# Two blocks of a transformer: x before the memory tokens at the start, and the second memory projection inside the waits of the normalizer and router

## What is computed

```python
for layer in range(2):
    mem_kv = mem @ w_mem_kv[layer]                # 256 memory tokens -> 256 key and 256 value columns
    h = x @ a_w_in[0]                             # layer 0: q, f_raw, i_in, g (768 columns each), qm (256)
    seq_out = hgrn2_mix(q, f_raw, i_in, g, ...)   # gated linear recurrence
    mem_out = memory_attention(qm, mem_k, mem_v)
    x = post_norm(x, concat(seq_out, mem_out) @ w_o[layer], ...)   # layer norm of 2**0.5 * x + y
    x = post_norm(x, hier_moe(x, ...), ...)       # top group of 4, top 2 experts of 4 in it
```

## Time and profile before

| | us |
|---|---|
| median of 3 runs | 1787.0 (1785.41 to 1790.78) |
| profiled execution, device time | 1784.4 |
| its span in the trace | 1782.7 |
| PE busy in it | 1706.0 (96%) |
| mean granted PE clock | 0.982 of full |

### The profile page before, as it was taken

How to read it: one execution, slowest core, us unless ns; L and a number is a source line. 1 busy time by engine, 2 the same in 40 slices (tenths; PEclk the granted TensorE clock), 3 DMA queues, 4 the chain that set the end, 5 groups by cost and what they waited for, 6 DMA issues and landing times.

```text
span 1782.7 us, 28889 instructions
## 1 busy us (share of the span) xinstructions
PE 1706.0 (96%) x11796; PEld 1569.2 (88%) x11796; DVE 1064.6 (60%) x1365; ACT 888.1 (50%) x1222; POOL 82.7 (5%) x127
## 2 busy tenths in 40 slices
PE   7999999999989999989999989999999999999998
PEld 6997799878977998779998978999899998989997
DVE  4775676878556668875445555555555556755454
ACT  4645446765554467644445654444544445444443
POOL 8000020003000200000000000000000000000000
PEclk9999999999989999999999999999999999999999
DMA  7530577974204779845553333555455554545552
GB/s 242 167 128 38 172 241 244 339 268 159 102 1 149 238 241 335 272 154 189 188 188 113 118 142 126 183 186 188 142 194 184 188 189 147 184 142 189 188 184 76
DMA packets 236750, 317.24 MB, mean 178 GB/s; under 512 B 5561, under 2 KB 210704, under 8 KB 236656
## 3 DMA queue, kind: packets, MB, share of 16 engines
q1 hardware_dynamic: 234080, 309.09, 52.7%
q0 software_dynamic: 2576, 6.83, 1.4%
HBM read 314.84 MB, written 1.06 MB: 177 GB/s over the span
## 4 chain that ended last, share of the span: by engine, by line
PE 87%; DVE 7%; ACT 3%; issue 1%; DMA 1%; SPq 0%; DVEq 0%; ACTq 0%
PE PB L371 17%; PE PB L372 17%; PE PB L373 17%; PE Y L371 7%; PE Y L372 7%; PE Y L373 7%; PE PB L555 2%; PE PB L556 2%; PE PB L557 2%; DVE LO L1504 2%; ACT HI L998 1%; PE Y L731 1%; PE PB L437 1%; PE PB L641 1%; DVE ST L1570 1%
## 5 line engine op out<-in xcount | busy, mean ns | idle before, releaser
L1504 DVE TENSOR_TENSOR LO<-RAW,HI 128x1024 fp32r<-128x1024 f32 (+2 forms) x498 | 582.0, 1214 | 301.2 <-ACT HI L998 300.6
L371 PE MATMUL PB<-XTH,HI 128*128 128x256 f32 x2128 | 609.4, 286 | 14.5 <-DVE XTL L1543 7.0
L372 PE MATMUL PB<-XTL,HI 128*128 128x256 f32 x2128 | 606.9, 285 | 0.0
L373 PE MATMUL PB<-XTH,LO 128*128 128x256 f32 x2128 | 606.6, 285 | 0.0
L998 ACT ACTIVATE HI<-RAW 128x1024 fp32r<-128x1024 f32 (+2 forms) x498 | 489.1, 1034 | 228.1 <-PE PB L373 173.3
L371 PEld LDWEIGHTS PB<-XTH,HI 128*128 128x128 f32 x2128 | 413.2, 194 | 19.6 <-DVE XTL L1543 8.1
L372 PEld LDWEIGHTS PB<-XTL,HI 128*128 128x128 f32 x2128 | 413.4, 194 | 1.6
L373 PEld LDWEIGHTS PB<-XTH,LO 128*128 128x128 f32 x2128 | 413.1, 194 | 0.0
L371 PE MATMUL Y<-HI,HH 128*128 128x512 f32 x384 | 150.2, 391 | 1.1 <-DVE HL L1514 1.1
L372 PE MATMUL Y<-LO,HH 128*128 128x512 f32 x384 | 150.0, 391 | 0.0
L373 PE MATMUL Y<-HI,HL 128*128 128x512 f32 x384 | 149.4, 389 | 0.0
(11 more groups left out here) (414 smaller groups left out, 2411.6 us busy)
## 6 DMA issues: line engine op xcount, KB each, us to landing
RAW<-in_ffn_pre_w_gate SPq DMA_DIRECT2D x22, 1024.0 KB, 5.3
RAW<-in_ffn_pre_w_up SPq DMA_DIRECT2D x22, 1024.0 KB, 5.3
RAW<-in_ffn_pre_w_down SPq DMA_DIRECT2D x22, 1024.0 KB, 4.8
RAW<-in_ffn_post_w_gate SPq DMA_DIRECT2D x22, 1024.0 KB, 5.3
RAW<-in_ffn_post_w_up SPq DMA_DIRECT2D x22, 1024.0 KB, 5.3
RAW<-in_ffn_post_w_down SPq DMA_DIRECT2D x22, 1024.0 KB, 4.8
AR<-in_w_gate SPq DMA_DIRECT2D x18, 1024.0 KB, 6.7
RAW<-in_w_down SPq DMA_DIRECT2D x18, 1024.0 KB, 5.3
```

The source lines that it names most:

```text
L371: pe.matmul(out_ap, ah, bh, start=start, stop=False)
L372: pe.matmul(out_ap, ah, bl, start=False, stop=False)
L373: return pe.matmul(out_ap, al, bh, start=False, stop=stop)
L1504: ins = dve.tensor_tensor(LO[:, slot, c], raw_of(n.u)[0][:, c], HI[:, slot, c].bitcast(F32), ALU.subtract)
```

## The change

x is loaded and transposed first, in two DMAs; the first weight unit is split ahead of x's evictions. The memory tokens are loaded behind the three f_raw units, and transposed two columns at a time (`mem_pair`) behind the second and third q unit, side unit 0 and side unit 1; the parameters follow side unit 2. Side units 7 and 8 are now w_mem_kv[0]. The two units of w_mem_kv[1] come behind w_o: half of the first in the normalizer's wait in place of 12 of 16 idle products, its other half and the second unit in the router's wait of layer 0 in place of the 15. ACT and DVE split these two units between the operations of the output projection. In both layers the gates are turned after the gather's fifth step, not its eighth.

```diff
 z_full sp_act sp_ready la_full ea_done am_ready so_full log_a
-rt_full r_dve r_act gt_ready gt_sb oh_ready gi_ready sel_ready xg_full xg_f xg_hi xg_lo gw_full gw_sb cnt_full ht_full st_ready yg_full yg_hi yg_lo y_last
+rt_full r_dve r_act gt_ready gt_sb oh_ready gi_ready sel_ready xg_full xg_f xg_hi xg_lo gw_full gw_sb cnt_full y_read mk_done ht_full st_ready yg_full yg_hi yg_lo y_last
 h_mul h_gb h_hi h_lo
...
     for t in range(NT):
-        sp.dma_start(XN[:, t, :], a["mem"][0, t * P:(t + 1) * P, :]).then_inc(s["mem_in"], 16)
-    load_cols(a["w_mem_kv"][0], 0, KC, 0, UC)
-    load_cols(a["w_mem_kv"][0], 0, KC, UC, UC)
-    sp.dma_start(X[:, :, :], a["x"][0].rearrange("(t p) n -> p t n", p=P)).then_inc(s["x_in"], 16)
+        sp.dma_start(X[:, t, :], a["x"][0, t * P:(t + 1) * P, :]).then_inc(s["x_in"], 16)
     for base in (MIX, 0, 2 * MIX):
...
             load_cols(a["a_w_in"][0], 0, KC, base + j * UC, UC)
+        if base == MIX:
+            for t in range(NT):
+                sp.dma_start(XN[:, t, :], a["mem"][0, t * P:(t + 1) * P, :]).then_inc(s["mem_in"], 16)
     load_cols(a["a_w_in"][0], 0, KC, 4 * MIX, UC)
...
         load_cols(a["a_w_in"][0], 0, KC, 3 * MIX + j * UC, UC)
+    load_cols(a["w_mem_kv"][0], 0, KC, 0, UC)
+    load_cols(a["w_mem_kv"][0], 0, KC, UC, UC)
+    load_rows(a["w_o"][0])
     load_cols(a["w_mem_kv"][1], 0, KC, 0, UC)
     load_cols(a["w_mem_kv"][1], 0, KC, UC, UC)
-    load_rows(a["w_o"][0])
     moe(0)
...
+    def cols_half(slot, j):
+        for k in range(KC):
+            w = slice(k * UC + j * P, k * UC + j * P + P)
+            mm = split_product(Y[:, 0, 512 + j * S:512 + (j + 1) * S], HI[:, slot, w], LO[:, slot, w],
+                               CTH[:, k, :], CTL[:, k, :], k == 0, k == KC - 1)
+        return mm
     def moe(layer):
...
         if layer == 0:
-            pe.matmul(Y[:, 1, 0:P], ONES[:, :], TRIL[:, :], start=True, stop=True)
+            pe.matmul(Y[:, 1, P:2 * P], ONES[:, :], TRIL[:, :], start=True, stop=True)
         stay_awake(3, Y[:, 1, 512:1024])
...
             for t in range(NT):
-                mm = pe.matmul(Y[:, 0, t * 512:t * 512 + 20],
+                mm = pe.matmul(Y[:, t, 0:20],
                                TMP[k // 2][:, (k % 2) * S + t * P:(k % 2) * S + (t + 1) * P], RWR[:, layer, k, :],
...
+        if layer == 0:
+            cols_half(mk_slot, 1).then_inc(s["w_used"], 1)
+            claim(0)
+            cols_N(0, **cols_T_mem)
         for b in range(4):
             claim(b, counted=False)
-        stay_awake(15)
+        if layer:
+            stay_awake(15)
         pe.wait_ge(s["sel_ready"], layer + 1)
...
-        gather(range(KC))
+        gather(range(5))
         pe.wait_ge(s["gt_ready"], layer + 1)
...
         mm.then_inc(s["rt_full"], 1)
+        gather(range(5, KC))
...
                 yclaim(1)
+                if layer == 0:
+                    pe.wait_ge(s["mk_done"], 1)
                 pe.wait_ge(s["gt_sb"], layer + 1)
...
     pe.wait_ge(s["ident"], 1)
-    transposes(XN, "mem_in", (32, 32))
     cols_T_mem = dict(xh=CTH, xl=CTL)
-    claim(0)
-    cols_T(0, new=True, **cols_T_mem)
-    claim(1)
-    cols_N(1, **cols_T_mem)
-    pe.wait_ge(s["par_in"], 16 * 12)
-    for b, rows_ in ((2, 70), (3, 85)):
+    transposes(X, "x_in", (32, 32))
+    def mem_pair(i, b):
         claim(b)
-        pe.transpose(PB[:, b, 0:rows_], SM[0:rows_, (b - 2) * P:(b - 1) * P], IDENT[0:rows_, 0:rows_])\
-            .then_inc(s["tp_full"], 1)
-    transposes(X, "x_in", (16, 16))
+        for t in range(NT):
+            for c in range(2):
+                mm = pe.transpose(PB[:, b, c * S + t * P:c * S + (t + 1) * P],
+                                  XN[:, t, (2 * i + c) * P:(2 * i + c + 1) * P], IDENT[:, :])
+        mm.then_inc(s["tp_full"], 1)
+    def parameters():
+        claim(2)
+        pe.wait_ge(s["par_in"], 16 * 12)
+        pe.transpose(PB[:, 2, 0:70], SM[0:70, 0:P], IDENT[0:70, 0:70])
+        pe.transpose(PB[:, 2, 70:155], SM[0:85, P:2 * P], IDENT[0:85, 0:85]).then_inc(s["tp_full"], 1)
     for j in range(6):
...
         cols_T(j % 4, new=j == 0)
+        if j == 4:
+            pe.wait_ge(s["lf_done"], 3)
+            pe.wait_ge(s["mem_in"], 32)
+            mem_pair(0, 2)
+        elif j == 5:
+            mem_pair(1, 3)
...
     side_unit(0)
+    mem_pair(2, 0)
     pe.wait_ge(s["q_ready"], 1)
...
             side_unit(m - 1)
+        if m == 2:
+            mem_pair(3, 1)
+        elif m == 3:
+            parameters()
         pe.wait_ge(s["m_high"], m - 1)
...
             level(m, [(j * P, blk(M, 2 * j), blk(M, 2 * j + 1)) for j in range(6)])
+    read(1)
     mem_scores(0, QM0, (0, 1))
...
     out_rows(first=3, between=mem_beside(0, PN0, PT0), ah=XTH, al=XTL)
-    renewed(16)
+    mk_slot = unit()
+    pe.wait_ge(s["y_read"], 1)
+    cols_half(mk_slot, 0)
+    renewed(4)
     moe(0)
...
         table(SILU_SET)
+        if layer == 0:
+            used()
+            act.activation(MK[:, 1, :, :], Y[:, 0, 512:1024], ACT.Copy).then_inc(s["mk_done"], 1)
+            used()
+            act.activation(MV[:, 1, :, :], PB[:, 0, :], ACT.Copy).then_inc(p_free[0], 1)
         gather_scaled(range(4))
...
     full = [(b, 2 * b, 512) for b in range(4)]
-    transposed(CTH, full)
-    split(RING)
-    used()
-    act.activation(MK[:, 0, :, :], PB[:, 0, :], ACT.Copy).then_inc(p_free[0], 1)
     split()
-    used()
-    act.activation(MV[:, 0, :, :], PB[:, 1, :], ACT.Copy).then_inc(p_free[1], 1)
-    split()
-    act.wait_ge(s["tp_full"], n.next("tp", 2))
-    act.activation(PV[:, 0:70], PB[:, 2, 0:70], ACT.Copy).then_inc(p_free[2], 1)
-    act.activation(PV[:, 70:155], PB[:, 3, 0:85], ACT.Copy).then_inc(p_free[3], 1)
     transposed(XTH, full)
+    split(RING - 1)
+    def mem_pair(i, b):
+        transposed(CTH, [(b, 2 * i, 512)])
+    def parameters():
+        act.wait_ge(s["tp_full"], n.next("tp"))
+        act.activation(PV[:, 0:155], PB[:, 2, 0:155], ACT.Copy).then_inc(p_free[2], 1)
...
             .then_inc(p_free[(3 + j) % 4], 1)
+        if j:
+            mem_pair(j - 1, 1 + j)
         split()
...
         else:
-            ins = act.activation((MK, MV)[j - 7][:, 1, :, :], PB[:, b, :], ACT.Copy)
+            ins = act.activation((MK, MV)[j - 7][:, 0, :, :], PB[:, b, :], ACT.Copy)
         ins.then_inc(p_free[b], 1)
...
     side_unit(0)
+    mem_pair(2, 0)
     def level_exp(m):
...
         side_unit(m - 1)
+        if m == 2:
+            mem_pair(3, 1)
+        elif m == 3:
+            parameters()
         if m == 8:
...
         mem_transposed(PT, (2, 3))
+        if k == 1:
+            split()
         act.wait_ge(s["ao_full"], k)
...
         used()
+        if k == 1:
+            split()
         n.v += 1
...
-        dve.wait_ge(s["x_ready"] if n.at("xr") else s["x_in"], n.at("xr") or 16)
+        dve.wait_ge(s["x_ready"] if n.at("xr") else s["x_in"], n.at("xr") or 32)
         for t in range(NT):
             tile_done(t, experts)
-            after(dve.scalar_tensor_tensor(out=XN[:, t, :], in0=X[:, t, :], scalar=ALPHA, in1=Y[:, t, :],
-                                           op0=ALU.mult, op1=ALU.add))
+            dve.scalar_tensor_tensor(out=XN[:, t, :], in0=X[:, t, :], scalar=ALPHA, in1=Y[:, t, :],
+                                     op0=ALU.mult, op1=ALU.add).then_inc(s["y_read"], 1)
+            dve.wait_ge(s["y_read"], n.next("yr"))
             for h in range(2):
...
-    def mem_and_rows(hi=CTH, lo=CTL):
+    def mem_and_rows(hi=CTH, lo=CTL, more=False):
         used()
...
         used()
+        if more:
+            split()
         mixed(6, PB[:, 0, :], hi, lo)
         used()
+        if more:
+            split()
...
         lg = sm(0, NT, 20)
-        after(dve.tensor_tensor(lg, Y[:, 0, :].rearrange("p (t e) -> p t e", t=NT)[:, :, 0:20],
+        after(dve.tensor_tensor(lg, Y[:, :, 0:20],
                                 bc(RB[:, layer, :].unsqueeze(1), NT, 20), ALU.add))
...
         if layer == 0:
-            after(dve.tensor_copy(IOTA[:, :], Y[:, 1, 0:P]))
+            after(dve.tensor_copy(IOTA[:, :], Y[:, 1, P:2 * P]))
...
+        if layer == 0:
+            n.v += 2
         split()
...
-    n.next("tp", 2)
-    transposed(CTH, CTL)
-    n.next("tp", 4)
-    split(RING)
-    for _ in range(2):
-        used()
-        split()
+    split()
     transposed(XTH, XTL)
-    n.next("tp", 4)
+    n.next("tp", 9)
+    split(RING - 1)
+    def mem_pair(i, b):
+        dve.wait_ge(s["tp_hi"], n.next("tph"))
+        rest(CTL[:, 2 * i:2 * i + 2, :], PB[:, b, :], CTH[:, 2 * i:2 * i + 2, :]).then_inc(p_free[b], 1)
     dve.wait_ge(s["pool_const"], 1)
...
         used()
+        if j:
+            mem_pair(j - 1, 1 + j)
         split()
...
     split()
+    mem_pair(2, 0)
...
             used()
+            if m == 2:
+                mem_pair(3, 1)
             split()
...
     mem_norms(PN0, (3,))
-    mem_and_rows(XTH, XTL)
+    mem_and_rows(XTH, XTL, True)
```

## The result

The changed kernel takes 1764.8 us (median of 4 runs, 1763.7 to 1767.5), against 1786.2 (1779.1 to 1790.8) for the kernel before in the same comparison: ratio 0.9886, 95% interval 0.9851 to 0.9921. The medians differ by 21.4 us, where 18.6 was forecast, and 1764.8 lies within the forecast's own spread, 1764 to 1772.

A forecast was written before the change was run, and what follows sets the result against it. PE was taken as the bound, busy 1706.0 of 1782.7 us. The terms summed to 18.6 us gained, from a median of 1787.0 to 1768; own spread 1764 to 1772, with (a) and (b) 1762 to 1776.

The forecast's parts named there:

- start, to the end of side unit 0: Kernel head: x's first projection starts at 14.15 us and ends at 21.45 against 39.37, +17.9 us gained.
- pair 2's remainder on the level chain: First level: DVE takes this remainder ahead of `differences`, on the chain ending PE's 0.68 us wait; -0.6 us.
- split ahead of the layer norm: Output projection: the second extra unit's split on DVE falls ahead of the layer norm; -0.6 us.
- router of layer 0, to the first expert product: Added projection starts the gather 4.6 us later, the first expert product at 216.7 against 213.97; -2.7 us.
- clock behind the gather, layer 0: First two expert units: without the 1.84 us gap no low clock follows; mean of two layers' losses, +2.0 us.
- the 7.3: Head: us from first product to release of ACT's MK copy in the old first unit, assumed for the new one.
- (a): Behind the gathers: the clock falls anyway, after twelve tiny products; gain 14.6 us, 1772; chance 0.22.
- (b): Layer 0's router: added work exposed whole, and pair 3's 2.1 us comes through; gain 15.3, 1772; chance 0.15.
- pair 3's 2.1: Level chain: pair 3's remainder makes DVE's LO 2.1 us later; forecast hidden, with 0.7 us to spare.
- (c): First units: DVE and ACT bound them, GpSimd's masks slowing LO by 8%; 1.5 us over three units, 1770; chance 0.04.
- (d): Start: no change, the weight stream holds it and PE waits for units instead of x; 1787; chance 0.03.
- (e): Ahead of the layer norm: slower, DVE stuck at the second w_mem_kv[1] unit's split; 1792 at 24 us late; chance 0.04.

The follow-up runs named there:

- run 4: The changed kernel executed once more, unaltered, on the same chip as the three follow-ups before it: 1764.75 us, ratio 0.9904 to the kernel before.
- run 9: The changed kernel with DVE's remainder of memory pair 2 moved behind the first `m_high` product: 1764.65 us, ratio 0.9887.
- run 7: The changed kernel with both halves of the first moved unit in the normalizer's wait, no idle products there: 1763.1 us, ratio 0.9883.
- run 2: The changed kernel with the gates turned after the gather's eighth step again, in both layers: 1770.6 us, ratio 0.9943.
- run 1: The kernel before with only the gates turned after the gather's fifth step, in both layers: 1775.9 us, ratio 0.9962.
- run 3: The changed kernel without the 96 products on the w_mem_kv[1] units, idle products instead: median 1764.9 us of four runs; two others took 2631 and 4206.
- run 5: The changed kernel without PE's claim of bank 0 ahead of layer 0's gather: 1764.9 us, ratio 0.9893.
- run 10: The changed kernel with no bank 0 claim, x's evictions first, both halves in the normalizer's wait, pair 2's remainder late: 1762.5 us, ratio 0.9872.
- run 6: The changed kernel with x's evictions ahead of the first unit's split on ACT and DVE: 1764.25 us, ratio 0.9884.
- run 8: The changed kernel with no bank 0 claim, x's evictions first and both halves in the normalizer's wait: 1763.0 us, ratio 0.9866.

## Why the prediction was right

Its terms against the profiled executions, each the change of the distance between two instructions.

| term | predicted | measured |
|---|---|---|
| start, to the end of side unit 0 | +17.9 | +16.7 |
| memory pairs 0 and 1 | -1.0 | -0.9 |
| pair 2's remainder on the level chain | -0.6 | -0.6 |
| parameters | -0.3 | -0.2 |
| split ahead of the layer norm | -0.6 | -0.7 |
| router of layer 0, to the first expert product | -2.7 | -2.6 in run 4; -6.9 here, with 4.3 of low clock |
| clock behind the gather, layer 0 | +2.0 | +1.5 |
| gates early, layer 1 | +1.9 | +2.1 |
| clock behind the gather, layer 1 | +2.0 | +2.7 |

With run 4's router they add up to 18.0, against 18.6 predicted. The profile after loses the 4.3 in its router, and gains 3.1 at places that the change doesn't touch: 2.3 between the first experts and layer 1's norm, where the granted clock averaged 0.98 against 0.97 before, and 0.9 behind layer 1. That makes 16.9. The 4.3 was in no term of the sum, and that 3.1 came back elsewhere is luck: over the twelve profiles the first of these places took 308.7 to 314.5 us and the second 1193.3 to 1197.3. The ratios of the two comparisons of this kernel, 0.9886 and 0.9904, make 20.4 and 17.1 us, to either side of 18.0.

**The start** was mis-sized by 1.2 us. PE started at 14.06 as forecast (14.15). But the prediction let the new first unit pay "the 7.3" of the old one. It took 22.64 - 14.06 = 8.6, since the granted clock stayed at 0.50 to nearly 20 us. The rule of the Trainium skill (TensorE: Matmul & The Clock Gate, "What's actually happening") that the array starts throttled is borne out again by the 0.55 of the first product. How long it stays so was not in the row of one execution: from the first product to the first eviction it took 7.5 us in run 9 and 8.8 in run 4, with the same work. (Run 9's profile gives a granted clock of 1.00 there, though its first product also took 0.55; so only its time is used.)

**The levels.** The wait for the scaled q is 0.61 where 1.05 stood, since pair 2's transposes now run in it. At the first `m_high` 0.84 stands where 0.68 stood. The prediction had said about 1.3: 0.68 and the 0.6 of pair 2's remainder. That is about what lies between the side unit and the level, but pair 3's four transposes at 67.55 fill part of it, as the prediction's own text on pair 3 had said. At the second `m_high` PE waits for nothing, as predicted. The level starts at 77.67, right behind the parameters, and its operand was ready at 76.4:
```profile
75.44 0.95 DVE L2042 TENSOR_TENSOR AR<-AR 128x768 f32<-128x768 f32 x1
```
So pair 3's remainder stayed hidden. Run 9 settles that pair 2's is the cause of the 0.6.

**The normalizer.** In the changed kernel's DVE timeline the split ends right where the layer norm starts, as predicted.
```profile
165.21 2.36 DVE L1558 TENSOR_TENSOR LO<-RAW,HI 128x1024 fp32r<-128x1024 f32 x2 [4.12 <-ACT HI L1037]
167.49 1.21 DVE L1621 SCALAR_TENSOR_TENSOR XN<-X,Y 128x1024 f32<-128x1024 f32 x1
```
DVE starts the norm 0.7 us later against PE, and PE has no more to do than before, so 0.77 us stay unfilled ahead of its transposes where 0.25 did. This is part of why run 7 gains.

**The router.** The placement was right: the projection costs 4.75 to 4.80 at the gather (4.6 predicted) and 2.64 at the expert unit, since the early gates take out the last split's wait.

**The clock behind the gathers.** The two units take 11.80 or 11.81 us in every one of the twenty places with early gates, so the gain of 1.5 + 2.7 is what the one profile of before had lost. That it came to the 4.0 of the sum is therefore partly luck. In run 2 one place of two with the same gap lost nothing, and the other 1.45.

**The rivals.** (a), a clock that falls behind the gather even without a gap, did not come: no kernel with early gates shows it, in twenty places. The gap was followed by a low clock in both layers of before and in layer 1 of run 2, not in layer 0 of run 2. The old head had such a place too: behind the 2.89 us ahead of x's transposes the granted clock was 0.50 to 0.54 from 30 to 33 us. (b) did not come either: the early gates take 2.1 of the router's 4.75 back, as priced, and pair 3's 2.1 does not come through. (c) is not seen: after 14.06, PE waits for no split in its first units. (d) and (e) are excluded by the ratio.

**What stays open.** No run has the new head alone: its gain is read as distances in the profiles, and only the gates, the projection, pair 2 and the small edits were changed singly. The low stretch in the first router is in the profiles of the changed kernel and of runs 1, 2, 3, 5 and 10, not in those of before and of runs 4, 6, 7, 8 and 9. It comes with the projection and without it, and in one of two executions of one program. What decides it, no run here shows. Whether runs 8 and 10 (0.9866 and 0.9872) really beat the change (0.9886 and 0.9904) stays open too: their 2 to 4 us show in the distances, but the intervals of the whole time overlap. Of run 3, the two executions of 2631 and 4206 us (mean granted clock 0.58 and 1.00) have no explanation here.

## What to carry to other kernels

An engine that must evict, copy and split at the end of a gather decides when the next weights are ready: move the small copy that waits longest ahead of the last split, and the gap goes whole, at 2 us a place. Work put into a filled wait costs what the idle products did not cover, and can be priced to some tenths by counting both. When an edit is worth 1 to 4 us in 1765, read it as a distance between two instructions at the same granted clock: a low stretch that comes and goes is worth as much.

## What the runs showed of the hardware that was not expected

The same program, executed twice, held a granted clock of 1.00 through its first router in one execution and 0.50 for much of it in the other (4.3 us), after the same work at full clock and the same 0.77 us wait. A gap of 1.85 us was followed by full clock in one layer and by a first product of 0.55 us in the other, in one execution. The first 1 MB unit of the new head landed 7.2 to 8.2 us after its issue in ten profiles, with the same transfers queued ahead of it.
